# A decoder block on eight cores: the gate, pooling and output matmuls of a slot put between the attention steps of the next slot

## The reference

```
h = rmsnorm(x, g1);  u | q | k | v | gate logits = h @ w_in        # 512|512|512|512|2048 columns
ya = causal_multiscale_pool(u) @ w_branch_a                        # windows 2, 4, 8, 16
q, k = rmsnorm per 64 channels
a = softmax(q1 k1 - slope*distance) - lam * softmax(q2 k2 - slope*distance)   # 4 heads, causal
yb = rmsnorm(a @ v) @ w_branch_b
x = x + (sigmoid(g0) * ya + sigmoid(g1) * yb) @ w_out
x = x + square(relu(rmsnorm(x, g2) @ w_ff1)) @ w_ff2               # 4096 hidden channels
```

## Time and profile before

| | us |
|---|---|
| median of 3 runs | 1930.6 (1925.36 to 2021.57) |
| profiled execution | 1920.41, its span 1918.9 (slowest core) |
| spans of the eight cores | 1913.0 to 1918.9 |
| projection, from 0 to 441.0 | 441.0 |
| attention, slots 3, 2, 1, 0, from 441.0 to 1050.4 | 244.2, 181.6, 116.8, 66.8 |
| p3a, from 1050.4 to 1481.7 | 431.3 |
| MLP, from 1481.7 | 437.2 |

### The profile page before, as it was taken

One profiled execution on the slowest core, in us unless ns is written; L12 is line 12 of the kernel. 1 busy time (PEld: TensorE's weight loads), 2 busy tenths in 40 slices (PEclk: granted clock), 3 DMA queues, 4 the chain that ended last, 5 costly groups with the idle time before them and its releaser, 6 DMA issues.

```text
span 1918.9 us, 33423 instructions; the slowest of 8 cores (1913.0 to 1918.9 us)
## 1 busy us (share of the span) xinstructions
PE 1634.8 (85%) x12240; PEld 981.9 (51%) x12240; DVE 620.8 (32%) x1137; ACT 989.8 (52%) x1472; POOL 103.2 (5%) x137
## 2 busy tenths in 40 slices
PE   2788888887999999999987797795861999999999
PEld 1344444446888877777776343342320444444444
DVE  1455444441110111113246643343310415142231
ACT  2466555658999999999996212120501304031120
POOL 1100000000000000000000221221200000000000
PEclk9899999998999999999999898988886999999999
DMA  6333222215655651020011212122156021120102
GB/s 178 126 100 100 88 89 88 88 40 87 92 90 96 144 89 35 2 89 2 2 60 45 88 35 98 66 66 99 44 192 209 27 77 56 45 88 23 66 1 77
DMA packets 47199, 148.11 MB, mean 77 GB/s; under 512 B 5664, under 2 KB 8096, under 8 KB 46656
## 3 DMA queue, kind: packets, MB, share of 16 engines
q1 hardware_dynamic: 41424, 119.53, 19.2%
q0 software_dynamic: 5616, 26.45, 8.6%
HBM read 155.63 MB, written 43.12 MB: 104 GB/s over the span
## 4 chain that ended last, share of the span: by engine, by line
PE 44%; ACT 32%; DMA 10%; issue 7%; DVE 4%; POOL 1%; ACTq 1%; SPq 1%; DVEq 0%; POOLq 0%
PE psum L173 44%; ACT arena L173 32%; DVE arena L173 4%; DMA arena<-xkv 3%; DMA arena<-w_b 3%; DMA arena<-w_in 2%; DMA x1s<-arena 1%; POOL arena L173 1%; ACTq L163 1%; DMA arena<-x1s 1%; SPq L173 1%; ACT L173 0%; DMA arena<-gq 0%; DVEq L163 0%; DMA arena<-gk 0%
## 5 line engine op out<-in xcount | busy, mean ns | idle before, releaser
L173 PE MATMUL psum<-arena 128*128 128x129 bf16 (+3 forms) x12240 | 1634.8, 291 | 280.2 <-DVE arena L173 162.2
L173 PEld LDWEIGHTS psum<-arena 128*128 128x128 bf16 x12240 | 981.9, 99 | 932.6 <-issue 397.3
L173 ACT ACTIVATE arena<-psum,arena 128x1024 bf16<-128x1024 f32 (+4 forms) x720 | 632.4, 948 | 248.1 <-PE psum L173 238.7
L173 ACT ACTIVATE arena<-psum 128x512 f32<-128x512 f32 (+2 forms) x292 | 171.9, 590 | 473.6 <-PE psum L173 443.4
L173 ACT ACTIVATE arena<-arena 128x1 f32<-128x1 f32 (+4 forms) x367 | 179.2, 496 | 128.9 <-DMA arena<-x1s 64.1
L173 DVE COPY arena<-psum 128x1024 bf16<-128x1024 bf16 (+4 forms) x178 | 109.5, 615 | 419.7 <-PE psum L173 410.7
L173 DVE SCALAR_TENSOR_TENSOR arena<-psum,arena 128x512 bf16<-128x512 f32 x208 | 147.4, 713 | 205.3 <-ACT arena L173 205.3
L173 DVE TENSOR_TENSOR arena<-psum,arena 128x512 f32<-128x512 f32 x128 | 87.9, 691 | 360.8 <-PE psum L173 200.5
L173 DVE SCALAR_TENSOR_TENSOR arena<-arena 128x128 f32<-128x128 f32 (+3 forms) x244 | 124.5, 512 | 149.4 <-ACT arena L173 107.8
L173 DVE TENSOR_SCALAR arena<-arena 128x128 f32<-128x128 f32 (+4 forms) x154 | 74.3, 483 | 65.3 <-ACT arena L173 55.4
L173 POOL TENSOR_TENSOR arena<-arena 128x512 bf16<-128x512 f32 (+3 forms) x48 | 62.4, 1300 | 251.7 <-DVE arena L173 250.3
(11 more groups left out here) (12 smaller groups left out, 13.6 us busy)
## 6 DMA issues: line engine op xcount, KB each, us to landing
arena<-xkv SPq DMA_DIRECT2D x96, 512.0 KB, 3.6
arena<-w_b SPq DMA_DIRECT2D x16, 1024.0 KB, 6.5
arena<-x1s SPq DMA_DIRECT2D x32, 512.0 KB, 4.1
w_b<-w POOLq DMA_DIRECT2D x8, 1024.0 KB, 9.8
w_b<-w POOLq DMA_DIRECT2D x16, 512.0 KB, 5.7
x1s<-arena SPq DMA_DIRECT2D x16, 512.0 KB, 2.8
out<-arena SPq DMA_DIRECT2D x16, 512.0 KB, 2.9
arena<-w_in SPq DMA_DIRECT2D x6, 1024.0 KB, 9.4
```

The costliest lines, as they stand in the source:

```text
L173: return lambda e: getattr(e, name)(*a, **k)
```

## The change

The host gives the weights in other layouts, so that each load is a contiguous row for each partition. Of `precast` only wp, w_a with w_b, w_o, w_1 and w_2 are left, 41 DMAs in all, one every 6 tiles of slot 3; the u and gate weights are loaded as f32, multiplied by the norm gain on VectorE and written back as bf16 (`fold_load`, `fold_mul`, ten times, 12 tiles apart). The transposed normalized own rows are written to DRAM in the projection (`hsp`) and loaded again (`load_hT`), in place of `p3a_norm`.

The work of p3a is cut into groups of up to 8 matmuls (`grp_u`, `grp_pm`, `grp_gate`, `grp_br`, `grp_out`), each with one accumulation in bank 7 and one evacuation. `pump` writes up to 1, 2, 4 or 8 of their matmuls behind each tile in slots 3, 2, 1 and 0. Slot 3's halo, u and pooling groups lie in slot 3 itself; its gates, branches and outputs and the u and pooling of slot 2 lie in slot 2's attention, and so on. Slot 0's gates, branches and outputs come after the attention (`drain_one`), over all banks. Sigmoid becomes Tanh of half the value, and the Ln and Exp of small norms become a power on GpSimd. Gate, branch and output weights go through three ring buffers, loaded again for each slot. w_1 is loaded during slots 1 and 0, half of w_2 at the end of the attention, the rest after the last output group.

```diff
+                    if r == 2:
+                        P.emit("sync", I("dma_start", out=hsp[g * 128:(g + 1) * 128, :].rearrange("p (k t) -> p k t", t=128),
+                                         in_=hT[:, :, 0:128]), reads=[th[0]], writes=[t_hsp[g]], stream="shs")
...
+        for r in range(0, 512, 32):
+            precast(w1_b[r:r + 32, :], w_1[r:r + 32, :], t_pc1, "pc1")
+        for r in range(0, 512, 32):
+            precast(w2_b[r:r + 32, :], w_2[r:r + 32, :], t_pc2, "pc2")
...
+        def load_hT(s):
+            th = lazy("hT3", o_hT3, 8192)
+            for b in range(4):
+                g = 4 * s + b
+                P.emit("sync", I("dma_start", out=hT3[:, :, b * 128:(b + 1) * 128],
+                                 in_=hsp[g * 128:(g + 1) * 128, :].rearrange("p (k t) -> p k t", t=128)),
+                       reads=[t_hsp[g]], writes=[th], stream="lht")
...
+        for s in (3, 2, 1, 0):
+            seq += [("fo", n) for n in range(8)]
+            seq += [("wo", 0), ("wu", 0), ("wo", 1)] if s > 0 else [("wo", 0), ("wo", 1)]
...
+        def pick():
+            return 7 if inattn[0] else nb()
...
+        def grp_u(s, g, wuv, wtok, after=None):
...
+                while k < POOL_W[g]:
...
+                    P.emit("pool", I("tensor_tensor", out=sb_[j][:, :, lo:144], in0=cur[:, :, lo:144], in1=cur[:, :, lo - k:144 - k], op=ALU.add),
+                           reads=[tcur], writes=[t_s[j]])
...
+        def grp_out(s, hf, blk, after=None):
...
+                P.emit("dve", I("scalar_tensor_tensor", out=xr[k], in0=bank(st["b"]), scalar=0.5, in1=xr[k], op0=ALU.mult, op1=ALU.add),
+                       reads=[tb[st["b"]]], writes=[T[f"xr{k}"]])
...
+                P.emit("sync", I("dma_start", out=x1s[r0:r0 + 128, hf * 512:(hf + 1) * 512], in_=xr[k]),
+                       reads=[T[f"xr{k}"]], writes=[t_x1d[s][blk]], stream=f"sx{s}")
+                if blk == 3:
+                    ring_next()
+                load_xr(n + 2)
...
+            return [us[0], o[(0, 0)], o[(0, 1)], grp_pm(0), us[1], o[(0, 2)], o[(0, 3)], grp_pm(1), us[2], o[(1, 0)], o[(1, 1)],
+                    grp_pm(2), us[3], o[(1, 2)], o[(1, 3)], grp_pm(3)]
...
+        def pump(budget):
+            if cool[0] > 0:
+                cool[0] -= 1
+                return
+            while budget > 0:
+                if cur_g[0] is None:
+                    if prio:
+                        prio.pop(0)()
+                        return
+                    if not fq:
+                        return
+                    cur_g[0] = fq.pop(0)
+                    cur_g[1] = 0
+                g = cur_g[0]
+                g["mms"][cur_g[1]]()
+                cur_g[1] += 1
+                budget -= 1
+                if cur_g[1] == len(g["mms"]):
+                    cur_g[0] = None
+                    g["fin"]()
+                    cool[0] = g["gap"] - 1
+                    return
...
+            P.emit("pool", I("tensor_tensor", out=rs, in0=rs, in1=mhalf, op=ALU.pow), reads=[t_rs, t_small], writes=[t_rs])
...
+        def load_w(which, q, j):
...
+            if tl_[q] is None:
+                tl_[q] = M.tok(o_[q], 16384, f"w{which}{q}")
+            P.emit("sync", I("dma_start", out=view(o_[q] + j * 4096, [2048], BF16), in_=src[q * 128:(q + 1) * 128, j * 2048:(j + 1) * 2048]),
+                   reads=[tok], writes=[tl_[q]], stream=f"lf{sn + q}")
...
+        BUD = {3: 1, 2: 2, 1: 4, 0: 8}
...
+            if i < NT - 1:
+                pump(BUD[tiles[i]["s"]])
...
+        for j in range(4):
+            load_w(1, 0, j)
+        for j in range(4):
+            load_w(1, 1, j)
...
+        for q in (2, 3):
+            for j in range(4):
+                load_w(1, q, j)
```

More of the change, by code:

```diff
@@ L384, in build_nc @@
         pend = []
+        t_hsp = [Tok(f"hsp{g}") for g in range(NG)]
         def flush_pend(keep):
@@ L548, in build_nc @@
[L548 to L558, removed]
@@ new lines, in G, with grp_halo, mk, f @@
+        def G(mms, fin, gap=1, pre=None):
+            return dict(mms=mms, fin=fin, gap=gap, pre=pre)
+        def grp_halo(g):
+            st = {}
+            def mk(kc):
+                def f():
+                    if kc == 0:
+                        st["b"] = pick()
+                    P.emit("pe", I("matmul", bank(st["b"])[:, 0:256], lhsT=wu3[:, kc, g * 128:(g + 1) * 128], rhs=hTh[:, kc, :],
+                                   start=(kc == 0), stop=(kc == 7)), reads=[T["wu"], t_hTh], writes=[tb[st["b"]]])
+                return f
+            def fin():
+                t = lazy("uh", o_uh, 4096)
+                P.emit("dve", I("tensor_copy", out=uh[:, g, :], in_=bank(st["b"])[:, 0:256]), reads=[tb[st["b"]]], writes=[t])
+            return G([mk(kc) for kc in range(8)], fin)
@@ new lines, in build_nc, with grp_gate, mk, f @@
+        rfo = {}
+        def grp_gate(s, fo, br, after=None):
+            st = {}
+            gi = (fo % 2) * 2 + br
+            def mk(kc):
+                def f():
+                    if kc == 0:
+                        st["b"] = pick()
+                        if br == 0:
+                            rfo[(s, fo)] = ring_use()
+                    k = rfo[(s, fo)]
+                    c0 = kc * 256 + br * 128
+                    P.emit("pe", I("matmul", bank(st["b"]), lhsT=ring[k][:, c0:c0 + 128], rhs=hT3[:, kc, :],
+                                   start=(kc == 0), stop=(kc == 7)), reads=[T[f"ring{k}"], T["hT3"]], writes=[tb[st["b"]]])
+                return f
+            def fin():
+                t = lazy(f"gt{gi}", o_gt[gi], 2048)
+                P.emit("act", I("activation", out=gts[gi], in_=bank(st["b"]), func=AF.Tanh, scale=0.5,
+                                bias=gbv[:, br * 8 + fo:br * 8 + fo + 1]),
+                       reads=[tb[st["b"]], T["gb"]], writes=[t])
+                if after:
+                    after()
+            return G([mk(kc) for kc in range(8)], fin, gap=2)
@@ L1156 @@
+        "gq": ca(np.tile(f(q_norm_g)[0], 2)[:, None]),
+        "gk": ca(np.tile(f(k_norm_g)[0], 2)[:, None]),
+        "lam": ca(np.tile(lamrow[None, :], (128, 1))),
+        "subg": ca(np.tile(f(subln_g)[0][None, :], (128, 1))),
+        "cst": cst,
     }
```

754 lines of the change are left out of this document (411 added, 343 removed).

## The result

The changed kernel takes 1953.8 us (median of 4, 1951.4 to 1957.0) against 1928.4 us of the kernel before: the ratio is 1.0138, interval 1.0112 to 1.0164. It is slower, by 1.4%: clear of noise, though inside the 2% that the prediction asks for, and far from the 1820 us that were forecast. In some executions, whatever the kernel, a die runs at a lower clock; the medians are over all executions, the ratios leave those out. The profiled execution took 1954.1, its span is 1952.5 us (core 7).

A forecast was written before the change was run, and what follows sets the result against it. TensorE was taken to become the bound of both attention and MLP. The attention's end at 1287, plus 55 for the last matmuls, 18, 437 for the MLP and 24, made 1821; forecast 1820 us, range 1700 to 1885.

The forecast's parts named there:

- explanation C: From the follow-ups, for the time over the forecast: added matmuls cost more than their own time in every tile.
- So POOL just keeps pace, and a pooling chain finds it on average half a cast late: 12 us: Slot 3: a cast takes 6.1 us against 6 tiles of 1.014; four poolings wait 3 us each.
- POOL's queue falls behind: Rival, slot 3: 41 casts of up to 8 us take 52 us more than the slot, about 1875; 0.14 with Tanh.
- the folding costs nothing while DVE has this room: Slot 3: 40 multiplications of 0.7 us on DVE, busy 28 of 244 us, cost nothing; 28 us without room.
- The pooling term: Slot 3: PE stands while copy, POOL adds and DVE subtraction run: 2.1 + 3.5 + 5.0 + 6.4 = 17 us.
- the u weights behind the four chained loads: Slots 2, 1, 0: u weights come 18.5 us after the last gate, branch groups cover part: 8, 11, 12 us lost.
- the waits overlap: Rival: the small waits in separate queues hide each other; 1713 us, band 1660 to 1770, chance 0.27.
- The head's end on VectorE: Slots 2, 1, 0: `fin1` holds DVE about 6 us at a head's end, delaying bank 7's evacuation: 3, 4, 8 us.
- The clock: Rival, slot 2 to last output: idle waits lower TensorE's granted clock; 2049 us at 0.74, chance 0.07.
- The MLP: Last stage: 2048 matmuls of 0.216 us make 442; the 437 us it took before were kept.
- the ring behind w_2: After the attention: eight w_2 loads precede the ring's next buffer in SP's queue; it lands at 32 us, 18 lost.
- x1s behind w_2: Early MLP: rows x1s stand behind eight more w_2 loads in SP's queue, ScalarE waits before the relus: 24 us lost.

The follow-up runs named there:

- all four edits: Changed kernel with two folding buffers, casts 12 tiles apart, loads not chained, and the pooling's last step on GpSimd with idle tiles in slot 3: ratio 0.9594.
- the fastest kernel: The kernel with all four edits, plus w_2 loaded later and the end of a head on VectorE cut in three: 1817.4 us, ratio 0.9424.

## Why the prediction was wrong

**The bound was right.** TensorE's work in slots 2, 1 and 0 was forecast as 212, 155.5 and 98.6 us; from the matmul records, counted by shape at their spacing at full clock, it is 212.7, 155.9 and 96.8 us (22 matmuls of slot 0 came after it). ScalarE fell to 197 of 262 us in slot 2. TensorE was busy for 88% of slot 2 and 86% of slot 1, though, where over 93% was the sign of being right. For explanation C little is left: slot 3 with all four edits takes 254 us, counted as before, against a sum of 247 by its tiles and added matmuls. Slot 2 in the fastest kernel takes 243 against 215, and there the idle time is not in every tile: 20 us of it stand in front of an added matmul behind a tile's own, in 34 of 149 places.

**The step that failed: "So POOL just keeps pace, and a pooling chain finds it on average half a cast late: 12 us".** The pace was wrong, and the place. A cast was put at 6.1 us by a row of the kernel before, so that the ten landings that stand in front of the second head's power would have taken 61 us. With the folding loads beside them they took 8.8 us each, 88 us from 527.3 to 615.7, while the norm asked for its power 72 us after the first of these casts. On the eight cores a cast took 7.9 to 8.9 us, and the power came 10 to 25 us late. The poolings, where I had put the 12 us, didn't find GpSimd late (below). The head's norm did, and the sum had no term for it, though the power is named in the rival. The casts spaced apart took 24 us off, and putting them back in the final kernel added 24 to 29. The rival "POOL's queue falls behind" named this mechanism and, with casts of up to 8 us, the pace; I gave it 0.14. Its 52 us for slot 3 stand against 42 measured, part of which has other causes.

**A second step failed beside it: "the folding costs nothing while DVE has this room".** It priced a queue by its busy time. VectorE had the room, 65 us busy of 314, but it stood 75.9 us in front of folding multiplications whose loads were on their way, and at two head ends the evacuation stood behind: 9.7 and 5.5 us on core 7. With the 18.5 us at the norm and the 14 us at half clock (below), and the 12 us taken off, that is 36 of the 42 us of slot 3.

**The pooling term** was right in place and size: 2.1, 3.5, 5.0 and 6.4 us forecast in slot 3, and the gaps of PE's matmul starts there are 2.8, 4.4, 4.0 and 6.5. It was in the forecast, so 17 of the 23 us that its removal gave are no part of the miss.

**Slots 1 and 0 came near their numbers in part by luck.** For the u weights behind the four chained loads I had 8, 11 and 12 us. The loads took what I said (18 us in slot 2, from the first issue at 907.6 to the landing at 925.8), but TensorE waited for them only 3.9 us in slot 2, not at all in slot 1 and 1.1 us in slot 0. For the ring's first load I had 5 us, and slot 2 shows no such wait. Against that, TensorE waited 21, 25 and 31 us for VectorE in the three slots, where bank 7, the poolings and the heads' ends had 11, 18 and 32. The rival "the waits overlap" was right about the u weights. In slot 2:

```profile
PE psum L173 <- DVE arena L173: 21.2, 17, 6.2
PE psum L173 <- DMA arena<-wub: 3.9, 1, 3.9
```

**The head's end on VectorE** was put at 3, 4 and 8 us for the four head ends of a slot together. A single gap in slot 2 is already twice its 3 us:

```profile
885.50 2.46 PE L173 MATMUL psum<-arena 128*128 128x512 bf16 x22 [0.46 <-DVE arena L173]
894.05 6.15 PE L173 MATMUL psum<-arena 128*128 128x512 bf16 x32 [6.09 <-DVE arena L173]
```

The split head end gave 25 us in all, mostly here: against the kernel with all four edits slot 2 is 12 us shorter (255 to 243), slots 1 and 0 are 5 and 8.

**The clock** was a rival of 0.07 and a partial truth. At each of the thirteen gaps of 5 us or more from slot 3 on, the granted clock falls to 1.2 GHz before the gap ends and stays there for some of the work behind it (0.50 of full speed from 602.7 to 623.2, around the longest gap of slot 3). Taking each matmul record in such stretches against its spacing at 2.4 GHz, 14 us are lost in slot 3, 7, 5.5 and 6 in slots 2 to 0 and 8 after. The forecast had these waits but no price for what follows them; that is 41 of the 131 us. It didn't decide by itself, as the rival would have it: with the waits gone the clock is back at 0.99 to 1.00.

**The MLP** was mis-sized by a border. The stage of 437 us begins at 1481.7, but its row counts 1952 wide matmuls, not 2048: 96 had run before, during the wait. I subtracted their 20.7 us a second time. From the end of the x1s wait to the end the forecast has 437 - 21 = 416 us, measured are 1952.5 - 1519.5 = 433. That is 17 of the 50 us in the last row; the 22 matmuls left over from slot 0 are 5, the last head's end, taken as hidden, 14 (two gaps of 6.4 and 7.5 us). With the 8 us at half clock, the ring 4 under and x1s 2 over their numbers, some 8 us of the 50 are left without a cause.

**Right in mechanism and size:** the ring behind w_2 and x1s behind w_2. The own rows in 256-byte pieces landed in 3.4 us for 256 KB where I took 3.9; the rule on small pieces (the Trainium skill, DMA: Bandwidth & Descriptors, Specifications), doubled as I had it, would have been wrong for the loads. The stores of such pieces are slower, 5.1 us for 256 KB against 2.5 for the 256 KB of x1s; but they run in the projection, beside its loads, and no run tells the pieces from that traffic.

```profile
x1s<-arena SPq DMA_DIRECT2D x32, 256.0 KB, 2.5
...
hsp<-arena SPq DMA_DIRECT2D x16, 256.0 KB, 5.1
...
arena<-hsp SPq DMA_DIRECT2D x16, 256.0 KB, 3.4
```

**Tanh** cost 1.3 us: the whole kernel has two table loads, one at its start and one in front of the first gate, and none where gates and Exps alternate (the group on the page, then the second load in ScalarE's timeline). That is as the Trainium skill's list of table sets has it (ScalarE: Activation LUTs, Table sets).

```profile
L173 ACT ACT_TABLE_LOAD x2 | 2.6, 1283 | 6.8 <-DMA arena<-xkv 6.7
```

```profile
772.21 1.28 ACT L173 ACT_TABLE_LOAD   x1
```

The forecast's 1820 us and the fastest kernel's 1817 agree by accident: that kernel is rid of waits which the forecast had counted. What stays open: slot 2 has 28 us over its sum even in the fastest kernel; where they stand is said above, but no run took them apart. And no run keeps the casts' traffic and takes only the power out from behind them.

## What to carry to other kernels

Price a step that is put into an engine's queue by the longest wait that may stand in front of it, not by the engine's busy share: a load's landing, a cast's landing, another engine's queue. Take a transfer's time with the traffic that the change itself adds, not from a row of the kernel before. Before moving matmuls under other work, take every instruction that waits for a transfer out of the queues that this work needs, or give it a distance longer than the transfer. A removed wait shows its worth only when the next one in the chain is gone too, so test pairs, and look whether the gap has only moved.

## What was not expected of the hardware

Loads issued side by side moved far more than in turn: with eight of 512 KB, the one of g2b and one of the ring in flight, eight slices of core 1 in a row (7 us) stand at 401 to 432 GB/s, where the kernel before had a mean of 200 GB/s in its last loads. The cores come to this stretch up to 21 us apart. Each has 324 to 408 GB/s in 8.5 us of it, and the two that come last, cores 1 and 6, have the most. The page of that stretch (1364 to 1400), in 40 slices:

```profile
DMA  0000685053999799999999999898400698967999
GB/s 2 0 0 9 155 228 191 0 18 86 269 209 209 282 401 341 410 419 414 405 428 432 401 414 371 259 396 362 171 20 0 96 398 341 328 241 246 307 369 360
```

By the profile GpSimd takes 1.03 us for a power over 128x4 values, almost as much as for an addition over 128x572 (1.14 us); the columns as in rows 3, over the whole kernel:

```profile
L173 POOL TENSOR_TENSOR arena<-arena 128x572 f32<-128x572 f32 x16 | 18.2, 1136 | 115.9 <-DVE arena L173 115.9
L173 POOL TENSOR_TENSOR arena<-arena 128x4 f32<-128x4 f32 x16 | 16.5, 1030 | 260.7 <-DVE arena L173 260.7
```
